# Two-layer encoder with routed experts: first weight blocks split in halves, the leading expert read from a minimum, the first selection and the last normalisation moved, row tables loaded later

## The reference, cut to what matters

```python
logits = (x @ w_router).astype(jnp.float32)
top_v, top_i = lax.top_k(logits, TOP_K)
gates = jax.nn.softmax(top_v, axis=-1)
combine = jnp.sum(jax.nn.one_hot(top_i, N_EXPERTS, dtype=jnp.float32) * gates[..., None], axis=-2)
for e in range(N_EXPERTS):
    out = out + combine[..., e:e + 1].astype(x.dtype) * swiglu(x, w_gate[e], w_up[e], w_down[e])
x = layer_norm(DEEPNORM_ALPHA * x + out, ln2_g[l], ln2_b[l])
```

## Time and profile before

| | |
|---|---|
| median of 3 runs | 1157.72 us (1156.75 to 1159.4) |
| the profiled execution: its own time / its span | 1161.09 us / 1159.2 us |
| busy in the span: TensorE, weight load, VectorE, ScalarE, GpSimd | 1115.8, 824.1, 642.5, 467.4, 44.2 us |
| moved by DMA | 300.07 MB, mean 259 GB/s |
| blocks of expert weights (gate, up, down) | 70, 70, 70 |

### The profile page before, as it was taken

One profiled execution on the slowest core, in us unless ns is written; L12 is line 12 of the kernel. 1 busy time (PEld: TensorE's weight loads), 2 busy tenths in 40 slices (PEclk: granted clock), 3 DMA queues, 4 the chain that ended last, 5 costly groups with the idle time before them and its releaser, 6 DMA issues.

```text
span 1159.2 us, 14644 instructions
## 1 busy us (share of the span) xinstructions
PE 1115.8 (96%) x5874; PEld 824.1 (71%) x5874; DVE 642.5 (55%) x742; ACT 467.4 (40%) x593; POOL 44.2 (4%) x45
## 2 busy tenths in 40 slices
PE   7899999999999999989999999999999999999995
PEld 6677878888877778776666676666666666666663
DVE  3787675545467876754655534554543465555334
ACT  4465543344335656143444423333333334433220
POOL 2000020000023000000000000000000000000001
PEclk9999999999999999889999999999999999999998
DMA  9933256555547500088999989899999989999952
GB/s 284 366 127 109 77 181 210 186 181 181 181 145 216 210 1 1 1 314 325 358 370 353 347 331 371 296 394 386 337 371 342 374 293 383 372 356 336 395 213 76
DMA packets 126781, 300.07 MB, mean 259 GB/s; under 512 B 4938, under 2 KB 7128, under 8 KB 126704
## 3 DMA queue, kind: packets, MB, share of 16 engines
q1 hardware_dynamic: 124304, 291.52, 69.4%
q0 software_dynamic: 2112, 6.87, 2.2%
q10 hardware_dynamic: 288, 0.63, 0.1%
HBM read 297.88 MB, written 1.12 MB: 258 GB/s over the span
## 4 chain that ended last, share of the span: by engine, by line
PE 87%; DMA 6%; DVE 3%; ACT 2%; issue 2%; SPq 0%; POOLq 0%; POOL 0%; DVEq 0%; ACTq 0%
PE bank L1517 23%; PE bank L1518 22%; PE bank L1575 12%; PE bank L1945 7%; PE bank L1603 6%; DMA raw<-in_w_in 3%; PE bank L1955 3%; PE bank L1682 3%; PE bank L1791 2%; PE bank L1776 1%; PE bank L1708 1%; PE bank L1925 1%; DMA raw<-in_moe_w_up 1%; ACT w_hi L712 1%; DMA raw<-in_moe_w_down 1%
## 5 line engine op out<-in xcount | busy, mean ns | idle before, releaser
L1371 DVE TENSOR_TENSOR w_lo<-raw,w_hi 128x2048 fp32r<-128x2048 f32 x84 | 192.5, 2292 | 278.5 <-ACT w_hi L877 278.5
L1517 PE MATMUL bank<-w_hi,xT_hi 128*128 128x512 f32 (+1 forms) x832 | 333.4, 402 | 10.3 <-ACT w_hi L877 3.3
L1518 PE MATMUL bank<-w_hi,xT_lo 128*128 128x512 f32 (+1 forms) x832 | 323.2, 390 | 0.0
L877 ACT ACTIVATE w_hi<-raw 128x2048 fp32r<-128x2048 f32 x84 | 160.6, 1912 | 246.6 <-PE bank L1575 140.4
L1517 PEld LDWEIGHTS bank<-w_hi,xT_hi 128*128 128x128 f32 x832 | 158.1, 190 | 78.6 <-issue 34.5
L991 DVE TENSOR_TENSOR w_lo<-raw,w_hi 128x2048 fp32r<-128x2048 f32 x63 | 144.2, 2290 | 108.7 <-ACT w_hi L712 108.4
L1518 PEld LDWEIGHTS bank<-w_hi,xT_lo 128*128 128x128 f32 x832 | 158.4, 190 | 29.3
L1575 PE MATMUL bank<-w_lo,xT_hi 128*128 128x512 f32 (+1 forms) x640 | 168.2, 386 | 0.0
L712 ACT ACTIVATE w_hi<-raw 128x2048 fp32r<-128x2048 f32 x65 | 124.6, 1918 | 102.4 <-PE bank L1575 45.9
L1575 PEld LDWEIGHTS bank<-w_lo,xT_hi 128*128 128x128 f32 x640 | 118.8, 189 | 24.4
L1517 PE MATMUL bank<-w_hi,hT_hi 128*128 128x512 f32 x312 | 124.6, 399 | 2.3 <-issue 2.3
(11 more groups left out here) (202 smaller groups left out, 1022.7 us busy)
## 6 DMA issues: line engine op xcount, KB each, us to landing
raw<-in_moe_w_gate SPq DMA_DIRECT2D x70, 1024.0 KB, 8.4
raw<-in_moe_w_up SPq DMA_DIRECT2D x70, 1024.0 KB, 8.6
raw<-in_moe_w_down SPq DMA_DIRECT2D x70, 1024.0 KB, 8.3
raw<-in_w_in SPq DMA_DIRECT2D x24, 1024.0 KB, 9.0
raw<-in_ffn_w_gate SPq DMA_DIRECT2D x11, 1024.0 KB, 5.1
raw<-in_ffn_w_up SPq DMA_DIRECT2D x11, 1024.0 KB, 5.1
raw<-in_ffn_w_down SPq DMA_DIRECT2D x11, 1024.0 KB, 4.9
raw<-in_w_out SPq DMA_DIRECT2D x8, 1024.0 KB, 5.9
```

The costliest lines, as they stand in the source:

```text
L877: nc.scalar.activation(w_hi[:, m % NH, :], raw[:, n % NR, :], ACT.Copy).then_inc(hi_done, 1)
L1371: nc.vector.tensor_tensor(w_lo[:, m % NH, :], raw[:, (BASE_MOE + load[at[o]]) % NR, :], w_hi[:, m % NH, :].bitcast(F32), ALU.subtract).the ...
L1517: nc.tensor.matmul(o, hi, wh, start=start, stop=False)
L1518: nc.tensor.matmul(o, lo, wh, start=False, stop=False)
```

## The change

- SP: block 0 and the first block of the leading expert are loaded in two halves of 512 KB. The first half raises a semaphore of its own, `first_in`. Token tile 1 is loaded behind block 1, not ahead of it.
- ScalarE and VectorE split these two blocks in halves (`first_split_hi`, `first_split_lo`); TensorE starts on the first half of `w_hi` and waits for the second half in the middle of its eight products.
- GpSimd: in the first layer `beta_mix` is issued once six units are used, the norm's gain and bias rows once nine are.
- VectorE: the key by which experts are sorted becomes -2 + large + active, times -8, plus the expert's number; its minimum is the leading expert's number and is written to `lead` ahead of the comparisons.
- The gate values, the keys and `select(0)` move into `first_selection`, run behind the first block's split of the trio (or ahead of the loops without a trio).
- ScalarE: one `Silu` of two numbers behind the exponential.
- TensorE: 13 idle products in place of 28 ahead of `routed`, and 8 inside the trio's body ahead of its first unit.
- VectorE: the trio's last two additions (tile 1 of the second large expert) leave the loop body; tile 0 is normalised ahead of them, tile 1 behind them.

The diff, cut to its core (`...` stands for the lines from L1342 to L1352, which are the same in `first_selection`):

```diff
@@ -122,6 +122,7 @@
 FIRST_UNITS = 3
+assert TOP * SEQ > NE * SMALL, "one expert at least is large, so that the first is"
 AHEAD = 3
@@ -512,14 +515,19 @@
       sp.dma_start(xtok[:, tt, :], x[0, tt * P:(tt + 1) * P, :]).then_inc(x_in[tt], 16)
-  def load(n, src, free=None):
+  def load(n, src, free=None, first=True):
       if free is not None:
       k = src.shape[1]
-      sp.dma_start(raw[:, n % NR, :].rearrange("p (k n) -> p k n", k=k), src).then_inc(raw_in[n % NR], 16)
+      to = raw[:, n % NR, :].rearrange("p (k n) -> p k n", k=k)
+      if n in (BASE_IN[0], BASE_MOE) and first:
+          sp.dma_start(to[:, 0:k // 2, :], src[:, 0:k // 2, :]).then_inc(first_in, 16)
+          sp.dma_start(to[:, k // 2:, :], src[:, k // 2:, :]).then_inc(raw_in[n % NR], 16)
+      else:
+          sp.dma_start(to, src).then_inc(raw_in[n % NR], 16)
   def columns(w, c, part, parts, width):
@@ -532,7 +540,7 @@
       for u in range(U_IN):
-          if l == 0 and u == 1:
+          if l == 0 and u == 2:
               load_tokens(1)
@@ -547,14 +555,14 @@
               load(BASE_FFN + len(cols) + i, row_pair(ffn_w_down[0], i))
-  def expert_block(n, e, kind, c, part, free=None):
+  def expert_block(n, e, kind, c, part, free=None, first=False):
       if kind == "down":
           src = w[0, bass.ds(e, 1), part * k:(part + 1) * k, c * CW:(c + 1) * CW]
-      load(n, src.rearrange("o (k p) n -> p (o k) n", p=P), free)
+      load(n, src.rearrange("o (k p) n -> p (o k) n", p=P), free, first)
   def expert_loads(units, order, e_large, e_small, off, off_l, again=None):
@@ -592,7 +600,7 @@
   for u, (kind, c, part) in enumerate(expert_units()[0:FIRST_UNITS]):
-      expert_block(BASE_MOE + u, leader, kind, c, part)
+      expert_block(BASE_MOE + u, leader, kind, c, part, first=True)
   sp.wait_ge(routed, 1)
@@ -687,7 +695,11 @@
       toeplitz(l)
+      if l == 0:
+          pool.wait_ge(unit_used, BASE_IN[0] + 6)
       pool.dma_start(row[:], beta_mix[l:l + 1, :].broadcast_to([P, D])).then_inc(beta_in, 16)
+      if l == 0:
+          pool.wait_ge(unit_used, BASE_IN[0] + 9)
       norm_rows(2 * l, ln1_g, ln1_b, l)
@@ -710,6 +722,15 @@
       nc.scalar.activation(w_hi[:, n % NH, :], raw[:, n % NR, :], ACT.Copy).then_inc(hi_done, 1)
+
+  HALVES = (slice(0, UNIT // 2), slice(UNIT // 2, UNIT))
+
+  def first_split_hi(n, times):
+
+      act.wait_ge(first_in, 16 * times)
+      nc.scalar.activation(w_hi[:, n % NH, HALVES[0]], raw[:, n % NR, HALVES[0]], ACT.Copy).then_inc(first_hi, 1)
+      act.wait_ge(raw_in[n % NR], 16 * (n // NR + 1))
+      nc.scalar.activation(w_hi[:, n % NH, HALVES[1]], raw[:, n % NR, HALVES[1]], ACT.Copy).then_inc(hi_done, 1)
   def static_split(n):
@@ -807,7 +828,7 @@
           act.dma_start(tab[:, P:], table[:, P:]).then_inc(consts_in, 16)
-          split_hi(0)
+          first_split_hi(0, 1)
           split_hi(1)
@@ -860,6 +881,7 @@
   nc.scalar.activation(e_diff[:], top[:, 1, :], ACT.Exp).then_inc(diff_exped, 1)
+  nc.scalar.activation(lam_exp[:], lam_exp[:], ACT.Silu)
   act.wait_ge(routed, 1)
@@ -867,6 +889,12 @@
       n, m = BASE_MOE + load[at[o]], BASE_MOE + o
+      if o == 0 and at is LARGE_AT["trio"]:
+          act.wait_ge(unit_used, m - NH + 1)
+          first_split_hi(m, 2)
+          return
+      if o == 0:
+          act.wait_ge(first_in, 32)
       act.wait_ge(raw_in[n % NR], 16 * (n // NR + 1) + use)
@@ -991,6 +1019,17 @@
+  HALVES = (slice(0, UNIT // 2), slice(UNIT // 2, UNIT))
+
+  def first_split_lo(n, times):
+
+      for half, (ready, count) in enumerate(((first_hi, times), (hi_done, n + 1))):
+          dve.wait_ge(ready, count)
+          h = HALVES[half]
+          ins = nc.vector.tensor_tensor(w_lo[:, n % NH, h], raw[:, n % NR, h], w_hi[:, n % NH, h].bitcast(F32),
+                                        ALU.subtract)
+      ins.then_inc(lo_done, 1)
+
@@ -1216,7 +1255,7 @@
           transposed(0, 0)
-          split_lo(0)
+          first_split_lo(0, 1)
           split_lo(1)
@@ -1309,8 +1348,10 @@
   link(nc.vector.tensor_scalar(active[:], count, 0.0, None, ALU.is_gt))
-  link(nc.vector.tensor_tensor(order[:], large[:], active[:], ALU.add))
+  link(nc.vector.scalar_tensor_tensor(order[:], large[:], -2.0, active[:], ALU.add, ALU.add))
   link(nc.vector.scalar_tensor_tensor(order[:], order[:], -float(NE), e8, ALU.mult, ALU.add))
+  link(nc.vector.tensor_reduce(counts[:, 0:1], order[:], AX.X, ALU.min))
+  nc.vector.tensor_copy(lead[:], counts[:, 0:1]).then_inc(led, 1)
   link(nc.vector.tensor_tensor(cmp, order[:].unsqueeze(1).broadcast_to([P, NE, NE]),
@@ -1318,7 +1359,7 @@
   link(nc.vector.tensor_reduce(work_f[:, 0:NE], cmp, AX.X, ALU.add))
-  nc.vector.tensor_copy(lead[:], work_f[:, 0:1]).then_inc(led, 1)
+  dve.wait_ge(led, 1)
   nc.vector.tensor_reduce(work_f[:, AT_KEY:AT_KEY + NE], cmp, AX.X, ALU.add)
@@ -1338,19 +1379,6 @@
-  dve.wait_ge(diff_exped, 1)
...
-  link(nc.vector.tensor_scalar(own_key, own_key, -1.0, None, ALU.add))
@@ -1364,9 +1392,33 @@
       ins.then_inc(sel_ready, 1)
+  steps_routed = steps[0]
+
+  def first_selection():
+
+      steps[0] = steps_routed
+      dve.wait_ge(diff_exped, 1)
+      link(nc.vector.tensor_scalar(gate[:, 2, :], e_diff[:], 1.0, None, ALU.add))
+      link(nc.vector.reciprocal(gate[:, 0, :], gate[:, 2, :]))
+      link(nc.vector.tensor_tensor(gate[:, 1, :], gate[:, 0, :], e_diff[:], ALU.mult))
+      nc.vector.tensor_tensor(first[:], first[:], gate[:, 0, :].unsqueeze(2).broadcast_to([P, NT, NE]), ALU.mult)
+      link(nc.vector.tensor_tensor(second[:], second[:], gate[:, 1, :].unsqueeze(2).broadcast_to([P, NT, NE]), ALU.mult))
+      link(nc.vector.tensor_tensor(comb[:, :, 0:NE], first[:], second[:], ALU.add))
+
+      dve.wait_ge(pos_psum, 1)
+      places = bank[:, 6, 0:NT * NE].rearrange("p (t e) -> p t e", e=NE)
+      own_key = key[:, :, 0:NE]
+      link(nc.vector.scalar_tensor_tensor(own_key, places, 1.0, chosen[:], ALU.add, ALU.mult))
+      link(nc.vector.tensor_scalar(own_key, own_key, -1.0, None, ALU.add))
+      select(0)
+
   def large_split(at, load, o, off, off_l):
       m = BASE_MOE + o
+      if o == 0 and at is LARGE_AT["trio"]:
+          first_split_lo(m, 2)
+          first_selection()
+          return
       dve.wait_ge(hi_done, m + 1 + off_l)
@@ -1434,7 +1486,7 @@
       n_units = len(units)
-      adds = additions(units)
+      adds = [a for a in additions(units) if units is not TRIO or a[0:2] != (n_units - 1, "L")]
       for o in range(min(AHEAD, len(at))):
@@ -1479,24 +1531,37 @@
       add_outputs(n_units)
-  select(0)
+  def last_additions(e):
+
+      made = added_at(TRIO, "L", 1, 1) + ADDED_0
+      dve.wait_ge(added, made)
+      for q in (2, 3):
+          add_large(e, q, 1, BASE_MOE + U_TRIO)
+
+  with dve.If(n_trio < 1):
+      first_selection()
   with dve.If(n_trio > 0):
   last_rows = raw[:, BASE_MOE % NR, :].rearrange("p (r d) -> p r d", r=2)
-  def final_norm():
-      steps[0] = steps_ahead
-      for tt in range(NT):
-          norm_sums(3, tt, acc[:, tt, :])
-          normalise(3, tt, acc[:, tt, :], last_rows)
+  def final_norm(tt):
+      norm_sums(3, tt, acc[:, tt, :])
+      normalise(3, tt, acc[:, tt, :], last_rows)
   steps_ahead = steps[0]
   with dve.If(more < 1):
+      e = dve.value_load(work[0:1, 1:2], min_val=0, max_val=NE - 1)
+      dve.wait_ge(added, added_at(TRIO, "L", 1, 1) + ADDED_0)
+      final_norm(0)
+      last_additions(e)
       dve.wait_ge(added, 20 + ADDED_0)
-      final_norm()
+      final_norm(1)
+  steps[0] = steps_ahead
   with dve.If(more > 0):
+      with dve.If(n_trio > 0):
+          last_additions(dve.value_load(work[0:1, 1:2], min_val=0, max_val=NE - 1))
       with dve.If(n_pair > 0):
@@ -1507,7 +1572,8 @@
       dve.wait_ge(added, n_trio * 20 + n_pair * 8 + n_rest * 4 + ADDED_0)
-      final_norm()
+      for tt in range(NT):
+          final_norm(tt)
         @block.tensor
@@ -1557,7 +1623,9 @@
                   tile_ready(tt, part)
-              if tt == tts[0]:
+              if tt == tts[0] and halves:
+                  pe.wait_ge(first_hi, 2)
+              elif tt == tts[0]:
                   pe.wait_ge(hi_done, n + g + 1 + off)
@@ -1567,6 +1635,8 @@
                   kt = part * nk + k
+                  if tt == tts[0] and halves and k == nk // 2:
+                      pe.wait_ge(hi_done, n + g + 1 + off)
                   with_hi(o, xh[:, kt, t], xl[:, kt, t], wh[:, k, :], kt == 0)
@@ -1668,10 +1738,14 @@
       wl = w_lo[:, slot, :].rearrange("p (k n) -> p k n", k=nk)
-      if tt == 0:
+      if tt == 0 and n == 0:
+          pe.wait_ge(first_hi, 1)
+      elif tt == 0:
           pe.wait_ge(hi_done, n + 1)
           kt = part * nk + k
+          if tt == 0 and n == 0 and k == nk // 2:
+              pe.wait_ge(hi_done, n + 1)
           with_hi(o, xT_hi[:, kt, t], xT_lo[:, kt, t], wh[:, k, :], kt == 0)
@@ -1893,7 +1967,7 @@
   nc.tensor.matmul(o[:, NE:2 * NE], before, chosen[:, 1, :], start=False, stop=True).then_inc(pos_psum, 1)
```

(8 more changed lines are left out.)

14 lines of the change are left out of this document (3 added, 11 removed).

## The result

| | before | after |
|---|---|---|
| median | 1157.76 us (4 runs, 1156.75 to 1159.4) | 1149.36 us (4 runs, 1148.73 to 1150.71) |
| ratio, 95% interval | | 0.9934 [0.9918, 0.9951] |
| the profiled execution: own time / span | 1161.09 / 1159.2 us | 1149.71 / 1147.8 us |
| mean granted clock over the span | 0.988 | 0.991 |

The change makes the kernel faster by 8.4 us, 0.7%. The forecast was 1146.2 with a range of 1143.0 to 1150.5. The side is right and 1149.36 lies in that range, but the point is 3.2 us too low, and the measured time lies outside the forecast's own range (1143.5 to 1148.5), in the part that was added for the rivals A and B. The two profiled executions stand 11.4 us apart, 3 us more than the medians. The forecast against the profiled execution was 1149.6, and it took 1149.71.

A forecast was written before the change was run, and what follows sets the result against it. TensorE, 87% of the chain, bounds the kernel, with savings at the start, experts' entry and tail: -3.3 - 4.2 - 4.0 = -11.5, giving 1146.2 us for the median; own range 1143.5 to 1148.5, 8-in-10 range 1143.0 to 1150.5.

The forecast's parts named there:

- A: Rival, experts' start: table loaded twice or not beside register reads, ScalarE 1.3 to 2.8 us later; 1148.5 us, chance 0.18.
- B: Rival: the start gives nothing; toeplitz transfers fill the queue or VectorE's 1.5 us is handed on; 1149.7 us, chance 0.15.
- Part 1: Kernel start: three broadcast tables leave the stretch awaiting block 6, TensorE restarts sooner; -3.3 us, between 0 and -5.
- Term (b): Start: moving the tables brings block 6's split from 42.67 to 40.16, -2.5 us, plus -0.8 from the slow stretch.
- Term (c): Start: GpSimd's waits delay `rms_a`, so VectorE stands 1.5 us; cost taken as 0, upper bound +1.5.
- Part 2: Experts' start: earlier issue, half landing and ScalarE's readiness let TensorE start sooner; -4.2 us, range -1 to -5.5.
- (a): Experts' start: `lead` from a minimum and a cast moves SP's issue from 496.54 to 495.47, -1.07 us.
- (b), (c): Experts' start: first half lands 3.8 us after issue; `Silu` brings the table load ahead of register reads; TensorE starts -2.5.
- (d): Experts' start: VectorE's register reads come earlier; TensorE waits 0.9 us for first `w_lo`; second block's cover is 0.4.
- (e): Experts' start, clock: unit 0's end moves -4.4 us at full clock, -3.0 with slow idle products; -4.2 taken.
- Part 3: Tail: tile 0's norm runs while TensorE still works, ahead of the last two additions; -4.0 us.
- D: Rival: the clock stays at 1.2 GHz in the experts' first units, making it slower; 1162.2 us, chance 0.03.

The follow-up runs named there:

- the tail alone: The kernel before with only the last two additions moved behind tile 0's norm; 1151.65 us, ratio 0.9957.
- the entry alone: The kernel before with only the router and experts' entry edits (`lead`, halves, `Silu`, moved selection, 13 and 8 idle products); 1155.69 us, ratio 0.9993.

## Why the prediction was right, and where its point failed

**The step that failed**, for the point if not for the range, is in the sum: "The profiled execution took 1161.09, 3.4 above the median of 1157.72: 1149.6 for it, 1146.2 for the median." It takes the 3.4 us as an offset that both kernels share. They were the bad luck of one execution, and partly the very stalls that the change was credited with removing: its restart at 48.80 stands 3.6 us behind the mean of the three other traces with the old start. The changed kernel's profiled execution stands 0.35 above its median. Take the difference away and 11.4 becomes 8.4. Seen from the parts it is the same error: the start and the entry were sized from this trace, the tail was not touched by it. The 1149.6 for the profiled execution met 1149.71 by luck, as the 1.3 us from the router show.

**Part 1, forecast -3.3, measured -1.3 (median) or -1.5 (eight traces against four).** Mechanism and place were right: the tables leave the queue, block 6's copy comes sooner. Its size came from 42.67 in the earlier trace rows, where three other traces with the old start have 38.0 to 40.0. In the changed kernel the copy follows ScalarE's work ahead of it without a wait, so on the other traces there was little to gain. Term (b) had this bound at 40.16, read from the late trace; it was 38.91. Term (a), nothing behind 36.63, can't be told apart: in the pair that product came at 34.95, but with the old start the three other traces have 35.03 to 35.60. Term (c): the hold is 1.76 (forecast 1.5), and its cost is 0.2, seen where `rms_a` was put first; it was taken as 0.

**Part 2, forecast -4.2, measured -2.7 at unit 0's end (-3.5 in the pair), -1.1 at the last row of products, and -0.8, between -2.9 and +1.4, by the median.** (a) 1.09 against 1.07 forecast. (b), (c) ScalarE was ready 1.85 behind the exponential's end, exactly as forecast, and ahead of the copy it was last in the pair, as said; the landing, seen where the copy waited for it, came 4.1 behind the issue against 3.8. (d) No wait for the second block's `w_lo`: right, and the run with the old order priced the new one at 1.6. The wait of 0.9 for the first block's did not come, because TensorE itself was 1.3 us late. (e) failed: the 8 idle products took 3.12 us, the slow alternative, and TensorE began at 497.40 with `w_hi` ready at 496.08. The prediction had that case at -3.0 and took the other. What it did not see is that then (a) and (c) are covered by idle products: each undone alone costs TensorE at most 0.3. Nor did it see that part of the gain is lost again at the gathers, by about 1.6: "this gain holds to the end if the blocks keep up" looked at the data alone, not at the clock.

**Part 3, forecast -4.0, measured -3.98 in the pair, 4.0 in every trace, -4.8 by the median of the tail alone.** The register read and branch lay beside other work, as taken.

The three parts by their medians are -1.3, -0.8 and -4.8, together -6.9, against -7.9 for all at once in another group: they add up within the intervals.

**The rivals.** A did not come: no table load is left in the loop, and the 1.28 us runs beside the reads. The load stands 0.02 us behind the exponential, so the drain of 1380 ns that the Trainium skill ("ScalarE: Activation LUTs", What ACT_TABLE_LOAD costs) adds to a switch is not seen here either; by it the first copy could not start 2.05 us behind the exponential's start, since 0.20, 1.28, 0.20 and the drain make 3.06. B was half right: the short rows did slow the queue, as holding one back showed, and the start gave 1.3, or 0.6 without the first trace, of 3.3. Its time (1149.7, where its own sum gives 1149.5) is nearer to the 1149.36 than the forecast is, but the entry's shortfall is as much of the reason. C and D did not come. D's clock of 0.66 in the experts' first 10 us did, for a few us only.

## What to carry to other kernels

When the profiled execution lies off the median, find out whether the stalls that a change removes are what put it there; a second trace of the kernel before, or the spread of the runs, is worth more than another decimal in the sum. Count a gain at full size only if it does not hang on when a DMA landed or when the clock fell: here the tail's 4.0 us, a pure reordering of one engine's queue, was the one term that every trace repeated. Follow a gain to the end of the kernel, not only to the end of the unit where it is made. Idle products ahead of real work can cover the improvements made before them: shorten them when the data comes sooner, and measure the two together.

## What the runs showed of the hardware

- One kernel on one chip has runs from 1151.8 to 1162.5 us, and the mean granted clock (0.985 to 0.995) orders them on the mean. In the traces the clock of 1.2 GHz comes in short stretches, not at the same places in each execution: behind some waits of 2 to 4 us, in the router, and in the experts behind unit 0 only at the gathers of 32 narrow products, with TensorE busy all through (0.68 in 875 to 880 us of the entry alone, behind a gather at 872.75). It fell at 13 of 40 of them. A stretch on dense work costs about 1.6 us, as behind the changed kernel's first gather (8.53 less 6.96), and 3.1 where it lasts twice as long, as in the entry alone (17.68 from unit 0 to unit 2, against 14.53).
- A table load runs beside the sequencer's register reads when it stands ahead of them (2.05 us from the exponential's start to the copy), and after them when it stands behind (3.33).
- A wait that the profile puts down to another engine can be register reads: VectorE's 3.17 us "for `w_hi`" is 3.02 us of reads and branches when nothing waits for `w_hi`.
